# A four-layer transformer on one core: the second stack's first norm as a factor, other orders around the splits

## The chip, the cores and the metric

The kernel runs on one core of a Trainium2 chip. The metric is the device time of one execution in microseconds (us); lower is better. A second time that stands here is the span of one profiled execution, from the first to the last instruction on the core.

Five engines work side by side, each in its own order: TensorE (PE; its weight loads are PEld), VectorE (DVE), ScalarE (ACT), GpSimd (POOL) and the queue that starts most transfers, SyncE (SP).

## The reference, cut to what matters

256 tokens of width 1024 go through two stacks of two layers each. All weights are float32.

```
for i in (0, 1):                       # first stack, DEPTH = 2
    mix = token_mixers(x, w_in[i], ...)          # two attentions, gates ga, gb, then w_out
    x = layer_norm(ALPHA * x + mix, ln1)
    ffn = hierarchical_moe(x, ...)               # 32 experts, 2 of them for each token
    ple = sigmoid(x @ w_ple_gate[i]) * (p[i] @ w_ple[i])
    x = layer_norm(ALPHA * x + ffn + ple, ln2)
for l in (0, 1):                       # second stack
    h = rms_norm(x, attn_norm[l])
    x = x + hybrid_mixer(h, w_in_2[l], ...)      # cq, mq, mk, mv, rq, rk, rv; gates g0, g1, g2, rg
    h = rms_norm(x, mlp_norm[l])
    x = x + squared_relu_mlp(h, w_mlp_up[l], w_mlp_down[l])
return rms_norm(x, final_norm)
```

`rms_norm(x, g)` is x times a factor of the token, rsqrt(mean(x*x) + eps), times g of the column. A product of it with a matrix is therefore the product of x*g with the matrix, times the factor of each token (row).

## The kernel before, in words

**Blocks and splits.** The weights come as blocks of at most 128x2048 numbers, 1 MB. SP starts each block's transfer (line 1045) into a free buffer: three rings, and at times parts of other tiles that are lent (H, V, PT, GT, and YA and YB, which are parts of A). SP works its list in order, so a transfer whose buffer is not free holds up all later ones. Each block but those of `w_exp_down` is then split into a high and a low half: ACT casts it to WSh (line 1971), DVE subtracts and writes WSl (line 1406), both in two pieces. PE multiplies high by high, high by low and low by high, three matmuls where one would do (`mm3`, line 1060 is the call of all of them). There are three pairs of WSh and WSl, so two blocks can be split ahead of the one that PE works on.

**The plan.** All engines walk the same list of steps, written by `Plan`; each picks its own part of each step. `take` puts the transfer and the split of a block and of up to two blocks that follow into the list (`limit` caps how many), then the step that uses it. Small DVE steps (`spare`: the top-k search of the index attention, the routing) are dealt out `pace` at a time behind each `take`, `lead` at a time ahead of it. `fill` puts deferred blocks (`todo`: mostly the gates) between parts of an attention, so that PE has matmuls while softmax runs.

**Activations** are kept transposed for PE: XTh and XTl, 8 chunks of 128 columns by 256 tokens. `turn_split` fills them: four groups of four PE transposes (line 1156), each of two chunks, go to a PSUM bank each; where the vector along the columns is only a scale (`SCALED`), ACT writes the high halves (line 2066) and DVE the low ones (line 1659); with scale and shift (`SHIFTED`: ln1, ln2, o2) the two engines share the scaled copies first, then split them. There are four banks in turn, and a bank is free when the step that reads it has been done by its owner.

**The end of the first stack** (layer 1): `scatter` adds the experts' output to X on DVE, with the statistics (lines 1387, 1389); `normed` of ln2 writes H; `overflow` is a branch (line 936) that is only entered when an expert has over 64 tokens: PE waits for the last addition, then compares; `spread` has PE broadcast gain and shift of ln2; `affine` (lines 1729, 1732) makes X from H on DVE; `load_c2` fetches rope tables. `normed` of attn takes statistics of X and writes H again (lines 1364 to 1379, POOL's power at 2208, then 1720 and ACT's 2097), `turn_split` of attn transposes that, and `wide` of cq (416 columns) begins the second stack. In its layer 1 the same `normed` and `turn_split` stand behind the last `mlp_down` block, whose four PSUM quarters are done by token half, then by column half.

**The second stack's projections** follow in the order cq, mq, ct's transposes, mk, q_up, kv_up, mv, QT's transposes, rv, KT's transposes (line 1139), rope of mq, rq, rope of rq, then the attentions mla, moba and ret with the gates between. The staged copies of the wide products are ACT's (line 1993).

**Attention of the first stack** (`attend`, diff): scores of token half 0, softmax (exponentials: ACT, line 2020), a `fill` of a gate block, then `mix` on DVE (lines 1561 to 1570), scores of half 1, transposes of half 0's probabilities (line 1183), softmax of half 1, and so on.

**Ahead of the experts**: `ln1` is normed right behind w_out, three `ple` products stand between it and its transposes; then six blocks of gate and router (`parts`) with the routing dealt out, `ranks` (PE counts, DVE lines 1808 to 1818), `slots` (DVE lines 1824 to 1836, the gather matrix G), `spread` and `affine` of ln1 for both token halves, eight `gather` products whose banks ACT empties (line 2115), and `tokens_of` for expert 0 (ACT 2122, DVE 1856). H, which `affine` reads, is then lent as the first buffer for the experts' weights: SP waits at that transfer for the `affine` of half 1. The late steps of the routing and `kept` (DVE lines 1769 to 1852) stand behind the last gather. Each expert is two split blocks, one `down` block that is not split (32 matmuls with 64 columns), and `turn_h` (transposes at line 1279, DVE 1869 to 1873, ACT 2136).

## Time and profile before

| | us |
|---|---|
| median of 3 runs | 2013.76 |
| lowest and highest | 2011.25, 2013.92 |
| the profiled execution's own time | 2016.33 |
| its span | 2014.2 |
| its mean granted TensorE clock | 0.975 of full |

A profile has a busy time for each engine, a chain of waits that ended last, and groups of instructions by line; the trace behind it has every instruction with its start, its length and, in brackets, how long its engine had been idle before it and who released it. Line numbers are those of the kernel before. Where PE has a gap, the row that ends it says whom it waited for; "issue" means that nothing in the profile held it.

### The profile page before, as it was taken

How to read it: one execution, taken by the hardware profiler on the slowest of the kernel's cores; microseconds unless marked ns; L12 is line 12 of the kernel's file. 1: busy time of each engine (PE TensorE's matmuls, PEld its weight loads, DVE VectorE, ACT ScalarE, POOL GpSimd, SP SyncE). 2: the span in 40 equal slices, each digit the busy share in tenths (PEclk: the TensorE clock that was granted, in tenths of full speed). 3: DMA queues.
4: the chain of work that ended last, by engine and by line, in shares of the span. 5: the costliest groups of instructions: out<-in, count | busy, mean ns of one | idle time of the engine just before them, and what ended most of it. 6: DMA issues, size and time to landing. Idle time of an engine off the chain costs nothing.

```text
span 2014.2 us, 31129 instructions
## 1 busy us (share of the span) xinstructions
PE 1908.9 (95%) x12576; PEld 1746.1 (87%) x12576; DVE 1406.5 (70%) x2285; ACT 1073.4 (53%) x1680; POOL 65.7 (3%) x78
## 2 busy tenths in 40 slices
PE   7899989999989999899998799999999999999998
PEld 6789879989878898799897689998998889998997
DVE  5876779888669767788886666676445666676444
ACT  5454557777544545677774445445444544444442
POOL 1000000000000000000000000000000000000001
PEclk9999989999899999899998899999999999999999
DMA  7426169999544252799993343445555343345552
GB/s 290 138 84 232 58 244 404 384 407 421 214 167 148 105 218 72 305 404 373 421 421 149 115 167 115 152 153 174 199 189 184 131 157 137 126 176 180 188 189 84
DMA packets 61049, 426.76 MB, mean 212 GB/s; under 512 B 6960, under 2 KB 7088, under 8 KB 11872
## 3 DMA queue, kind: packets, MB, share of 16 engines
q1 hardware_dynamic: 59760, 421.65, 55.5%
q8 instruction: 104, 1.70, 0.3%
q0 software_dynamic: 416, 1.81, 0.3%
q10 hardware_dynamic: 720, 1.19, 0.2%
q14 instruction: 49, 0.40, 0.1%
HBM read 423.58 MB, written 1.05 MB: 211 GB/s over the span
## 4 chain that ended last, share of the span: by engine, by line
PE 78%; DVE 13%; ACT 4%; DMA 3%; issue 1%; POOL 1%; DVEq 0%; ACTq 0%; SPq 0%; POOLq 0%
PE bank L1060 63%; PE scp L1060 10%; DVE WSl L1406 4%; ACT WSh L1971 1%; PE bank L1279 1%; PE bank L1156 1%; ACT SC L2020 1%; DMA PT<-wts 1%; DMA H<-wts 1%; PE bank L1139 1%; DVE sm L1554 1%; POOL sm L2208 1%; PE bank L1183 1%; PE bank L1299 1%; DMA A<-wts 1%
## 5 line engine op out<-in xcount | busy, mean ns | idle before, releaser
L1406 DVE TENSOR_TENSOR WSl<-ring,WSh 128x1024 fp32r<-128x1024 f32 (+3 forms) x512 | 590.3, 1197 | 203.4 <-ACT WSh L1971 202.1
L1971 ACT CAST WSh<-ring 128x1024 fp32r<-128x1024 f32 (+3 forms) x512 | 499.2, 1029 | 191.0 <-PE bank L1060 98.2
L1060 PE MATMUL bank<-XTh,WSh 128*128 128x256 f32 x1216 | 349.6, 288 | 7.2 <-DVE A L1589 4.4
L1060 PE MATMUL bank<-XTl,WSh 128*128 128x256 f32 x1216 | 345.9, 284 | 0.0
L1060 PE MATMUL bank<-XTh,WSl 128*128 128x256 f32 x1216 | 345.8, 284 | 0.0
L1060 PE MATMUL bank<-WSh,FA 128*128 128x512 f32 (+1 forms) x848 | 303.5, 391 | 6.2 <-DVE FA L1863 6.1
L1060 PE MATMUL bank<-WSl,FA 128*128 128x512 f32 (+1 forms) x680 | 263.2, 387 | 0.0
L1060 PEld LDWEIGHTS bank<-XTh,WSh 128*128 128x128 f32 x1216 | 234.9, 193 | 9.6 <-issue 5.4
L1060 PEld LDWEIGHTS bank<-XTl,WSh 128*128 128x128 f32 x1216 | 235.2, 193 | 0.2
L1060 PEld LDWEIGHTS bank<-XTh,WSl 128*128 128x128 f32 x1216 | 234.9, 193 | 0.0
L1060 PE MATMUL bank<-WSh,XTh 128*128 128x512 f32 (+4 forms) x544 | 204.2, 375 | 14.3 <-DVE WSl L1406 11.1
L1060 PE MATMUL bank<-WSh,XTl 128*128 128x512 f32 (+4 forms) x544 | 201.4, 370 | 0.0
L1060 PE MATMUL bank<-WSl,XTh 128*128 128x512 f32 (+4 forms) x544 | 201.4, 370 | 0.0
L1060 PEld LDWEIGHTS bank<-WSh,FA 128*128 128x128 f32 x848 | 158.0, 190 | 39.4 <-DVE FA L1863 7.7
L1060 PE MATMUL scp<-WSh,FA 128*128 128x512 f32 x512 | 159.3, 389 | 0.0
L1060 PEld LDWEIGHTS bank<-WSl,FA 128*128 128x128 f32 x680 | 129.1, 190 | 24.2
L1060 PEld LDWEIGHTS bank<-WSh,XTh 128*128 128x128 f32 x544 | 105.1, 193 | 30.1 <-DVE WSl L1406 11.3
L1060 PE MATMUL bank<-FA,WSh 128*128 128x256 f32 x640 | 118.2, 287 | 0.0
L1060 PEld LDWEIGHTS bank<-WSh,XTl 128*128 128x128 f32 x544 | 104.8, 193 | 14.1
L1060 PEld LDWEIGHTS bank<-WSl,XTh 128*128 128x128 f32 x544 | 105.1, 193 | 13.4
L1060 PEld LDWEIGHTS scp<-WSh,FA 128*128 128x128 f32 x512 | 96.1, 188 | 19.9
L1060 PEld LDWEIGHTS bank<-TMP,ring 128*128 128x128 f32 x896 | 104.3, 192 | 2.2
(285 smaller groups left out, 2906.8 us busy)
## 6 DMA issues: line engine op xcount, KB each, us to landing
ring<-wts SPq DMA_DIRECT2D x264, 1024.0 KB, 4.9
V<-wts SPq DMA_DIRECT2D x40, 1024.0 KB, 12.4
PT<-wts SPq DMA_DIRECT2D x30, 1024.0 KB, 9.1
H<-wts SPq DMA_DIRECT2D x28, 1024.0 KB, 9.5
GT<-wts SPq DMA_DIRECT2D x12, 1024.0 KB, 13.2
A<-wts SPq DMA_DIRECT2D x8, 1024.0 KB, 7.5
ring<-wts SPq DMA_DIRECT2D x8, 584.0 KB, 7.1
ring<-wts SPq DMA_DIRECT2D x4, 832.0 KB, 7.7
```

The lines of the kernel that those rows point to most:

```text
L1060: return nc.tensor.matmul(dst, lhsT, rhs, start=start, stop=stop)
L1139: last = nc.tensor.transpose(bank[u % 4][0:s.w, j * P:(j + 1) * P], src, ident)
L1156: last = nc.tensor.transpose(bank[u % 4][:, j * P:(j + 1) * P], src(t, c), ident)
L1183: last = nc.tensor.transpose(bank[u % 4][:, (j - s.first) * P:(j - s.first + 1) * P], p_at(j // nk)[:, j % nk * P:(j % nk + 1) * P], ident)
L1279: last = nc.tensor.transpose(bank[u % 4][:, f * P:(f + 1) * P], SE[s.e % 2][:, f * P:(f + 1) * P], ident)
L1299: last = nc.tensor.transpose(bank[u % 4][:, j * P:(j + 1) * P], YC[:, 4 * s.n + j, s.j * P:(s.j + 1) * P], ident)
L1406: nc.vector.tensor_tensor(lo[:, c], buf[:, c], hi[:, c].bitcast(F32), ALU.subtract).then_inc(*lo_done.inc(("block", i)))
L1554: nc.vector.tensor_reduce(mx[:, h], scp[:, h, 0:kl], AX.X, ALU.max).then_inc(*dve_done.inc())
L1971: nc.scalar.copy(hi[:, c], buffers[s.buffer][:, c]).then_inc(*hi_done.inc(("half", i, k)))
L2020: ins = nc.scalar.activation(SC[:, h, 0:kl], scp[:, h, 0:kl], ACT.Exp, bias=nb[t][:, h:h + 1], scale=SCALE[s.name], accum_out=zs[t][:, h:h ...
L2208: nc.gpsimd.tensor_tensor(var, var, const("nhalf")[:, 0:groups], ALU.pow).then_inc(*pool_done.inc(("pow", *name)))
```

## The change

- **The factor.** For the second stack, `normed` and the scaled H are gone from the way into cq. In layer 0, `at0` transposes the H of ln2 and applies ln2's gain and shift times the attn gain (made by a step `columns`); in layer 1, `attn` transposes X itself. The factor of the tokens (`rms`) is computed beside the products and applied by ACT in its staged copies. `affine` of ln2 is put around the first cq block.
- **A second set of transposes.** The gates can't take a factor of the tokens, as they are made transposed; so a step `scaled` writes X times the factor to H (DVE half 0, ACT half 1), and after rq `at2` transposes H and refills XT for all that follows. KT's transposes move behind it, rope of mq ahead of rq.
- **mlp_down** of second-stack layer 0 ends by column half, then token half; the statistics of its additions move into `rms`.
- **overflow**: PE's and ACT's waits move inside the branch. `load_c2` no longer waits for `affine`.
- **keep_on**: four 256-column matmuls whose result is not used, ahead of the last `down` of each expert stage.
- **Slots and mixing**: `mix` of half 0 goes ahead of the fill; the splits of expert 0's blocks go behind `slots`; `affine` of ln1 is parted, half 1 behind the fourth gather and expert 0's first `tokens_of`; the late routing and `kept` go behind `turn_h` of expert 0; two `ple` products and their copies go ahead of ln1's `normed`, one stays behind it; `pace` is 3, not 8, during dv.

```diff
@@ Plan @@
+        self.ahead(i, spec)                # in take(); the body of ahead() is take()'s own loop, unchanged
...
+    def keep_on(self, n):
+        self.add("keep_on", n=n, u=self.bank("pe"))
...
         if att == "diff":
-            self.fill(fills[0])
             self.add("mix", name=att, l=l, t=0)
-        else:
-            self.fill(fills[0])
+        self.fill(fills[0])
...
         self.columns("w_in", "dk", l, W1["dk"], 512, src)
         self.add("rope", name="dq", l=l)
+        self.pace = 3
         self.columns("w_in", "dv", l, W1["dv"], 512, src)
...
-        self.add("normed", name="ln1", l=l, n=D)
+        self.limit = 0
         i = self.take(("w_ple", (l,), 0, 2, 0, D))
+        self.limit = 3
...
-        for c in range(3):
+        for c in range(2):
             ple(c)
+            ple_out(c)
+        self.add("normed", name="ln1", l=l, n=D)
+        self.ahead(i, self.specs[i])
+        ple(2)
         xt = self.use("XT", "pe")
-        ple_out(0)
-        ple_out(1)
...
+            self.limit = 0 if c >= 4 else 3
             blocks[c]()
...
         self.add("slots", l=l, i=i, p=self.use("P", "pe"))
+        self.limit = 2
+        self.ahead(len(self.specs) - 1, self.specs[-1])
+        self.limit = 3
         self.add("spread", name="ln1", l=l, scp=self.use("scp", "dve"))
-        self.affine("ln1", l)
+        self.affine("ln1", l, (0,))
...
-            if k == KD - 1:
-                for n in ROUTE_LATE:
...
-                self.add("kept", l=l)
+            if k == 3:
+                self.affine("ln1", l, (1,))
...
             self.add("turn_h", l=l, e=e, u=self.bank("dve"))
+            if e == 0:
+                for n in ROUTE_LATE:
...
+                self.add("kept", l=l)
             self.spread_out(1)
         self.pace = 1
+        self.keep_on(4)
         self.down(l, NE - 1)
@@ second_layer @@
-        self.add("normed", name="attn", l=l, n=D)
-        self.turn_split("attn", l, KD, xt=self.use("XT", "pe"))
-        for f in self.wide(w, "cq", l, 0, W2["cq"], W2["mq"] - W2["cq"], src):
-            f()
+        xt = self.use("XT", "pe")
+        self.turn_split("attn" if l else "at0", l, KD, xt=xt)
+        blocks = self.wide(w, "cq", l, 0, W2["cq"], W2["mq"] - W2["cq"], src)
+        if l == 0:
+            self.add("spread", name="ln2", l=DEPTH - 1, scp=self.use("scp", "dve"))
+            self.affine("ln2", DEPTH - 1, (0,))
+            blocks[0]()
+            self.affine("ln2", DEPTH - 1, (1,))
+            self.add("rms", l=l)
+        else:
+            self.add("rms", l=l)
+            blocks[0]()
+        blocks[1]()
...
         self.columns(w, "rv", l, W2["rv"], 512, src)
+        self.add("rope", name="mq", l=l)
+        self.add("scaled", l=l)
+        blocks = self.wide(w, "rq", l, 0, W2["rq"], 512, src, xt=xt)
+        blocks[0]()
+        blocks[1]()
+        self.turn_split("at2", l, KD, xt=self.use("XT", "pe"))
+        src = ("at2", l)
         self.turn("KT", l, 16, 96)
-        self.add("rope", name="mq", l=l)
-        self.columns(w, "rq", l, W2["rq"], 512, src)
@@ PE @@
+                elif s.kind == "keep_on":
+                    bank_free(u)
+                    for _ in range(s.n):
+                        last = mm(bank[u % 4][:, 0:256], ident, CST[:, 0:256], True, True)
...
                 elif s.kind == "overflow":
-                    for v in range(u - 4, u):
-                        pe.wait_ge(emptied(v), "bank", v)
-                    pe.wait_ge(dve_done, "added", "moe", l, 1, 1)
-                    overflow_tensor(e, l, yes)
+                    overflow_tensor(e, l, yes, u)
@@ DVE @@
+                elif s.kind == "rms":
+                    if l:
...
+                    for t in range(T):
+                        if l == 0:
+                            dve.wait_ge(dve_done, "affine", "ln2", DEPTH - 1, t)
+                        norm_stats(X[:, t:t + 1, :], 1, D, 160 + 2 * t, NORM_EPS, True, ...)
+                elif s.kind == "scaled":
+                    dve.wait_ge(pool_done, "pow", "attn", l, 0)
+                    nc.vector.tensor_scalar(H[:, 0, :], X[:, 0, :], RMS[:, 0, 1:2], None, ALU.mult)...
@@ ACT, staged copies of the wide products @@
-                        nc.scalar.copy(STAGED[s.name][:, t, ...], bank[u[t] % 4][:, 0:s.n])...
+                        dst, scale = STAGED[s.name][:, t, ...], 1.0
+                        if s.src[0] == "attn":
+                            act.wait_ge(pool_done, "pow", "attn", l, t)
+                            scale = RMS[:, t, 1:2]
+                        nc.scalar.activation(dst, bank[u[t] % 4][:, 0:s.n], ACT.Copy, scale=scale)...
```

## Rows read from the trace of the kernel before

**Rows 1.** The chain of waits that ended last: its share by engine (page)
```profile
PE 78%; DVE 13%; ACT 4%; DMA 3%; issue 1%; POOL 1%; DVEq 0%; ACTq 0%; SPq 0%; POOLq 0%
```

**Rows 2.** PE's waits over the span: engine, line, waited for: us in total, times, longest
```profile
PE bank L1183 <- DVE SC L1570: 5.3, 2, 2.6
PE bank L1060 <- DVE A L1589: 4.4, 1, 4.4
PE bank L1156 <- ACT GT L2104: 3.7, 2, 1.8
```

**Rows 3.** Stretches at the lower clock: length, busy time of each engine, granted clock, DMA
```profile
286.30:293.10 6.80, 4.34 (x12) 3.29 (x13) 6.07 (x9) 2.72 (x4) 0.00 (x0) 0.50 1.01 425
535.50:545.70 10.20, 9.43 (x46) 9.24 (x45) 2.25 (x3) 3.33 (x5) 0.00 (x0) 0.50 0.17 65
1078.20:1091.80 13.60, 12.57 (x58) 12.41 (x59) 3.34 (x6) 4.12 (x7) 0.00 (x0) 0.50 0.33 138
1102.10:1122.50 20.40, 7.56 (x30) 7.22 (x31) 14.01 (x31) 6.22 (x12) 2.86 (x5) 0.50 0.06 15
1562.90:1569.70 6.80, 4.16 (x19) 4.16 (x20) 3.73 (x13) 4.33 (x10) 1.30 (x2) 0.50 0.00 0
```

**Rows 4.** PE into the second stack's layers: start, length, operation, idle before
```profile
1104.96 2.07 PE L1060 MATMUL scp<-PR,PICK 128*128 128x256 f32 x8 [4.97 <-DVE H L1722]
...
1117.01 3.65 PE L1156 MATMUL bank<-CST,H 128*128 128x128 f32 x16 [9.98 <-ACT H L2097]
...
1565.54 3.65 PE L1156 MATMUL bank<-CST,H 128*128 128x128 f32 x16 [6.44 <-ACT H L2097]
```

**Rows 5.** PE's branch, and PE behind it at first-stack layer 0's end
```profile
L936 PEldq COMPARE_BRANCH  x2: 3421/3454/3486, 556.0 to 1101.5; - x2
...
559.68 1.09 PE L1156 MATMUL bank<-CST,H 128*128 128x128 f32 x4 [5.15 <-ACT H L2100]
562.62 2.82 PE L1156 MATMUL bank<-CST,H 128*128 128x128 f32 x12 [1.86 <-issue]
...
566.61 0.29 PE L1060 MATMUL bank<-WSh,XTh 128*128 128x292 f32 x1
```

**Rows 6.** ACT and DVE filling XT, affine, the copies ahead of mk
```profile
1118.13 3.40 ACT L2066 ACTIVATE XTh<-bank,PC 128x256 fp32r<-128x256 f32 x8 [0.66 <-PE bank L1156]
...
1119.01 3.43 DVE L1659 SCALAR_TENSOR_TENSOR XTl<-bank,PC,XTh 128x256 fp32r<-128x256 f32 x8 [2.94 <-ACT XTh L2066]
...
1106.32 1.22 DVE L1729 SCALAR_TENSOR_TENSOR X<-H,scp 128x1024 f32<-128x1024 f32 x1 [2.21 <-PE scp L1060]
...
1111.17 1.27 DVE L1364 BATCH_NORM_STATS2 sm<-X 128x6 f32<-128x512 f32 x2
...
1144.24 0.47 PE L1060 MATMUL bank<-WSh,XTh 128*128 128x512 f32 x1 [2.01 <-ACT A L1993]
```

**Rows 7.** SP ahead of the experts: its wait, the first transfer behind it, both layers
```profile
SPq L1045 <- DVE X L1732: 33.3, 2, 17.1
...
276.57 0.33 SPq L1045 DMA_DIRECT2D H<-wts  x1
...
819.64 0.33 SPq L1045 DMA_DIRECT2D H<-wts  x1
```

**Rows 8.** The same stretch on DVE, ACT and PE
```profile
809.05 2.36 DVE L1406 TENSOR_TENSOR WSl<-A,WSh 128x1024 fp32r<-128x1024 f32 x2 [0.53 <-ACT WSh L1971]
...
816.06 3.53 ACT L2115 ACTIVATE A<-bank,PC 128x512 f32<-128x512 f32 x4 [1.91 <-PE bank L1060]
...
824.38 2.01 ACT L1971 CAST WSh<-H 128x1024 fp32r<-128x1024 f32 x2 [0.65 <-DMA H<-wts]
...
832.68 0.79 PE L1060 MATMUL bank<-WSh,FA 128*128 128x512 f32 x1 [2.11 <-DVE FA L1863]
```

**Rows 9.** A down block at the lower clock (the last) and at full clock
```profile
1078.47 7.06 PE L1060 MATMUL bank<-TMP,PT 128*128 128x64 f32 x32 [1.87 <-DVE TMP L1873]
...
295.16 3.68 PE L1060 MATMUL bank<-TMP,ring 128*128 128x64 f32 x32
```

**Rows 10.** KT's or QT's transposes: an ACT copy of one group
```profile
1174.70 0.58 ACT L2030 COPY A<-bank 96x512 f32<-96x512 f32 x1
```

**Rows 11.** One step of the top-k search on DVE; PE's first product behind it
```profile
85.60 0.42 DVE L1537 MAX8 sm<-TMP 128x8 f32<-128x256 f32 x1
...
95.01 0.43 PE L1060 MATMUL bank<-XTh,WSh 128*128 128x256 f32 x1 [4.43 <-DVE A L1589]
```

**Rows 12.** Layer 0's diff attention: last exponential, the split that follows, softmax of half 1
```profile
110.27 0.21 ACT L2020 ACTIVATION_READ_ACCUMULATOR SC<-scp,sm 128x1 f32 x1
...
111.45 2.36 DVE L1406 TENSOR_TENSOR WSl<-ring,WSh 128x1024 fp32r<-128x1024 f32 x2 [2.51 <-ACT WSh L1971]
...
116.57 0.69 DVE L1552 TENSOR_TENSOR scp<-scp,CST 128x512 f32<-128x512 f32 x1
```

More of the change, by code:

```diff
@@ L181, in take, with ahead @@
         self.specs.append(spec)
+        self.ahead(i, spec)
+        self.spread_out(self.pace)
+        return i
+    def ahead(self, i, spec):
         order = self.order
@@ L196, in take @@
                 self.give_back(j)
-        self.spread_out(self.pace)
-        return i
     def release(self, i):
@@ L247, in turn_split @@
         pairs = range(2 * at, 2 * at + n, 2)
-        if name not in ("ln1", "ln2", "o2"):
+        if name not in ("ln1", "ln2", "at0", "o2"):
             for j in pairs:
@@ L473, in first_layer @@
                 self.down(l, e - 1)
+            if e == NE - 1 and l == DEPTH - 1:
+                self.add("columns")
             if e == NE - 1:
@@ L498, in first_layer @@
             self.turn_split("ln2", l, KD, xt=self.use("XT", "pe"))
-        self.add("spread", name="ln2", l=l, scp=self.use("scp", "dve"))
-        if l == DEPTH - 1:
-            self.affine("ln2", l)
+        if l < DEPTH - 1:
+            self.add("spread", name="ln2", l=l, scp=self.use("scp", "dve"))
     def down(self, l, e):
@@ L868, in build @@
                  "ct": (CTS, lambda t, c: CS[:, t, c * P:(c + 1) * P]),
[L869 to L871 removed]
+                 **{n: (XT, lambda t, c: H[:, t, c * P:(c + 1) * P]) for n in ("ln1", "ln2", "at0", "at2")},
+                 **{n: (XT, lambda t, c: X[:, t, c * P:(c + 1) * P]) for n in ("attn", "mlp")}}
+        SCALED = {"oa": lambda l, c: col("diff_subln_g", l, 0), "attn": lambda l, c: col("attn_norm_2", l, c), "at2": lambda l, c: col("attn_norm_2", l, c),
                   "mlp": lambda l, c: col("mlp_norm_2", l, c),
@@ L933, in overflow_pool, with overflow_tensor @@
                 pool.wait_ge(over[l]["dve"], "end", l)
-        def overflow_tensor(e, l, yes):
+        def overflow_tensor(e, l, yes, u):
             with e.If(yes > 0):
                 pe, o_pe = Waiter(e), over[l]["pe"]
+                for v in range(u - 4, u):
+                    pe.wait_ge(emptied(v), "bank", v)
+                pe.wait_ge(dve_done, "added", "moe", l, 1, 1)
                 def free(n):
@@ L1101, in tensor_program @@
                         if t == T - 1:
-                            names += [("read", i)] + ([("FA", s.fa)] if s.name == "w_out" and s.h else [])
+                            names += [("read", i)] + ([("FA", s.fa)] if s.name == "w_out" and s.h else [("XT", s.xt)] if s.name == "rq" and s.h else [])
                         if names:
@@ L1144, in tensor_program @@
                         pe.wait_ge(dve_done, "x_out", DEPTH + l, s.j // 2)
-                    elif s.name in ("ln1", "ln2", "attn"):
+                    elif s.name == "attn":
+                        for t in range(T):
+                            pe.wait_ge(dve_done, "y", "mlp", l - 1, s.j // 2, t)
+                    elif s.name == "at2":
+                        pe.wait_ge(dve_done, "scaled", l)
+                        pe.wait_ge(act_done, "scaled", l)
+                    elif s.name == "at0":
+                        pe.wait_ge(dve_done, "normed", "ln2", DEPTH - 1, s.j // 2)
+                        pe.wait_ge(act_done, "normed", "ln2", DEPTH - 1, s.j // 2)
+                    elif s.name in ("ln1", "ln2"):
                         pe.wait_ge(dve_done, "normed", s.name, l, s.j // 2)
@@ L1329, in tensor_program @@
                     ends = s.q == 3 and s.c == 3
-                    for n, t in [(n, t) for t in range(T) for n in range(2)] if ends else [(n, t) for n in range(2) for t in range(T)]:
+                    for n, t in [(n, t) for t in range(T) for n in range(2)] if ends and l == DEPTH - 1 else [(n, t) for n in range(2) for t in range(T)]:
                         for k in range(2):
@@ L2225, in gpsimd_program @@
                     power(4, 64, ("weighted", s.name, l, t))
+                elif s.kind == "rms":
+                    for t in range(T):
+                        power(1, 160 + 2 * t, ("attn", l, t))
                 elif s.kind == "normed":
@@ L2242, in gpsimd_program @@
                 elif s.kind == "load_c2":
-                    pool.wait_ge(dve_done, "affine", "ln2", DEPTH - 1, 1)
+                    pool.wait_ge(pe_done, "scatter", DEPTH - 1, 1, 1)
                     e.dma_start(CST[:, C_N:C_N + C2_N], consts[P * (C_N + C1_N):P * (C_N + C1_N + C2_N)].rearrange("(p n) -> p n", p=P)).then_inc(
```

62 lines of the change are left out of this document (45 added, 17 removed).

## The prediction

> **What bounds the kernel now.** I read the chain of waits first: PE has 78% of it, DVE 13%, ACT 4% [rows 1]. The end is set by PE's stream of products and by the places where DVE or ACT hold it. So I went through PE's gaps with their releasers [rows 2, 4, 5], then the stretches at half clock [rows 3] and at what a product loses there. Last I read SP's wait ahead of the experts [rows 7], because the change moves a step that this wait hangs on. About 0.2% (4.0 us) is what a measurement of this kernel can tell from no change.
>
> The sum is made on the profiled execution, 2016.33 us, which lies 2.57 above the median; it is taken off at the end.
>
> **1. dv's pace.** In layer 0 DVE works through top-k steps (0.46 each with the replace, [rows 11]) while PE waits 4.4 for its copies [rows 2]. Some 11 fewer stand ahead of them: the copies come right behind the split, 2.4 earlier, and the block behind the gap no longer starts at half clock (0.43 for a product that later takes 0.28, [rows 11]): 1.5. In layer 1 eight left-over steps fall ahead of other copies: +0.8. Together -3.1; ends: both gaps closed, -5.9, or the steps only moved, +1.
>
> **2. Mixing ahead of the fill.** PE's two 2.6 waits are for DVE's mixing of half 0 [rows 2]. The last exponential ends at 110.5, DVE is then idle until the split at 111.45 and starts softmax of half 1 at 116.57 [rows 12]. With mixing (some 2.9) first, split second, softmax comes at 115.8, 0.75 earlier, and then ACT's exponentials of half 1 are what is late next. So -0.75 in each layer, -1.5. Ends: both waits gone, -5.3; the split delays PE as much as it gains, +1.
>
> **3. ln1.** Two ple copies go ahead of the norm, so ACT's XT copies stand behind one, not three: the 1.8 waits for ACT [rows 2] shrink by 0.7 each, -1.4. Ends -3.6 and 0.
>
> **4. Slots, affine, routing.** `slots` no longer waits behind a split (2.36, [rows 8]), but two casts of 2.0 on ACT and two splits of 2.36 now stand ahead of ACT's gather copies and of `affine`. The first four gather copies, which end at 819.6 [rows 8], end near 822.0; tokens_of takes 0.5, `affine` of half 1 2.4 [rows 6]. SP issues the H transfer straight behind that `affine` (819.64, [rows 7]), so now at 825.0, 5.4 later; everything queued behind it on SP waits as long. Expert 1 starts 13.0 behind that issue (832.68, [rows 8]): transfer, cast at 824.38 [rows 8], splits; 1.6 of it was late routing ahead of the splits, which leaves: +3.7. The late routing (2.8) now stands behind `turn_h` of expert 0, where the next splits wait for it: +0.7. Layer 1: +4.5. In layer 0 the issue goes from 276.57 [rows 7] to 281, the routing gives back 1.9: +3.2, of which a shorter wait at `ranks` is part. Together +7.5. Ends: DVE's and SP's slack absorb it, 0; nothing absorbs it and the clock falls besides, +16. I take the middle because expert 1 already starts on a DVE wait [rows 8]: there is no slack at its own place, but 30 experts follow in which SP can only win time back where it waits for buffers.
>
> **5. keep_on.** Ahead of the last `down` PE idles 1.87 and then runs it at 0.50: 7.06 against 3.68 [rows 9]; the stretches are 10.2 and 13.6 long [rows 3]. Eight passes of some 0.21 (half of a 0.43 for the same width at half clock, [rows 11]) fit into that idle time, so they cost nothing; were the gap shorter, they would cost 1.7. If the clock holds, -3.4 in layer 1 and, by the same rows, -2.4 in layer 0: -5.8. Ends: -5.8 and 0. Both falls begin at that gap, so I take the full effect, and give the other its own case.
>
> The Trainium skill, "TensorE: Matmul & The Clock Gate", section "Why this matters for your kernels", has the clock fall only behind waits a good deal longer than this one. The trace shows falls that begin at 1.9 of idle, so it does not agree; by the rule those eight passes change nothing, and this term is 0. That is rival (b).
>
> **6. The branch.** PE's compare takes 3.42 to 3.49 [rows 5], behind DVE's last addition. It now starts when the scatter's products end, 1.5 earlier (554.5, not 556.0); the 5.15 idle in layer 0 [rows 5] shrinks, -1.3 (the 1.86 of "issue" behind it, code arriving, stays). Ends -1.5, 0. In layer 1 it lies inside term 7.
>
> The Trainium skill, "Advanced Engine Details and Errata", section "Control Flow Timing", gives a compare-and-branch about 108 ns. The trace has 30 times that. By the page this term would be 0.
>
> **7. Into the second stack, layer 0.** Now 4.97 idle, 2.07 of spread, 9.98 idle, then the transposes, 3.65, at half clock [rows 3, 4]: PE waits for spread, four `affine` parts of 1.2 (1106.32, [rows 6]), statistics (1.27 from 1111.17, [rows 6]) and scaling. After: the transposes follow on ln2's H itself, near 1105, and are written in the form with a shift, which in layer 0 took 559.68 to 566.61 with a hole of 1.9 [rows 5]: 5.1 to 5.6, so the first product comes at some 1110.6, not 1120.3 (3.3 behind the transposes' start at 1117.01). From there to mk, now at 1144.24 behind a wait for ACT's copy [rows 6], are 23.9. That stretch grows: DVE's `affine` halves (4.9 by [rows 6]) and the statistics now lie in it among the splits, and ACT's copies of cq wait for the factor; I put 3.3 of it on PE, two thirds of the `affine`. mk starts near 1137.8: -6.4. Ends: all 9.7 and the 2.0 wait in part, -10.8; -5.
>
> **8. Layer 1.** Statistics, power and scaling cost 6.44 idle [rows 4], at half clock [rows 3]. The transposes of X need none: they start at 1559.1. The stretch of 6.8 at half clock ends earlier, but the factor must be there for ACT's first copy, some 6 later, which it is. -7.1. Ends: 6.44 plus 1.7 of clock, -8.1; -5.5.
>
> **9. at2.** 16 more transposes are 1.83 at full clock (half of 3.65, [rows 4]). They cost more than that: ACT's eight copies take 3.40, DVE's eight 3.43 [rows 6], and the last low half ended 5.4 behind the first transpose, 4.9 at full clock. KT's groups, which used to lie between rv and rq with work beside them, now wait for those banks; their last copy (0.58, [rows 10]) ends some 5.9 behind the start of at2, and the scores wait for it. KT's own 1.9 is gone from its old place: +4.0 in each layer, +8.0. Ends: PE time alone, +1.9 each; 5.5 each and 1.7 of clock, +14.4.
>
> **10. Small.** Scaled ACT copies where exposed: +0.3. `scaled` (DVE 1.0, ACT 1.3 by its width, the affine row's 1.22), `columns`, `load_c2`: beside rv's and rq's products; without that cover some 1.3 per layer.
>
> **Sum**: -3.1 -1.5 -1.4 +7.5 -5.8 -1.3 -6.4 -7.1 +8.0 +0.3 = -10.8; 2005.5 on the profiled time, **2003.0** against the median.
>
> **Rivals.** (a) *Larger gain.* at2 costs its PE time only (4.2 less) and both mixing waits close (3.8 less): 18.8 off, 1995.0. For it: DVE is off PE's chain through most of rq. Against: the bank order ahead of the scores.
> (b) *keep_on buys nothing*, as the clock falls for a reason that lies ahead of the gap (the 10.2 and 13.6 stretches include `down`'s small products, [rows 3], where PE is busy 92%): the sum is -5.0, 2008.8. For it: idle of 1.9 occurs in many places with no fall. Against: both falls start at that very gap.
> (c) *Slower.* The experts pay in full: H's issue 5.4 late, routing 2.8 and a longer stretch at half clock as in 286.3 to 293.1 [rows 3], 1.7 to 3.4: 9.9 to 11.6 in each layer, 19.8 to 23.2 in place of 7.5: 2015.3 to 2018.7. It decides from 18.3 in both. For it: SP's list is in order, and it already waits 17.1 and 16.2 there [rows 7]. Against: in layer 0 `ranks` gives 1.5 back, and the routing had stood in expert 0's way before.
>
> **Chances**: forecast 0.48, (a) 0.20, (b) 0.22, (c) 0.06, the rest 0.04 spread about. Faster than 2009.7: all of the first two and over half of (b), 0.81; slower than 2017.8 only in (c) and odd mishaps, 0.06; else 0.13. The bounds that stand widest are terms 4 (8.5), 9 (6.4) and 5 (5.8) upward, 4 (7.5), 7 and 9 (4.3 each) downward; in few cases all go together: 1993.5 to 2011.5, which leaves out most of (c).
>
> **What the changed kernel's profile would show.** Term 5: `down` of expert 31 at 3.7 and no stretch at 0.50 there. Term 9: PE waits for ACT or DVE at KT's transposes and at the first scores, some 4 in all. Term 4: H's transfer some 5 behind the old place, and expert 1 late by 3 to 4. Terms 7 and 8: no wait on H; a wait for ACT's staged copies ahead of mk. Term 1: 2.0 left of the 4.4. Wrong would be: experts delayed by over 9 per layer, at2's block over 6, or a new wait of PE for the factor in cq's banks.

## The result, and the profile after

The changed kernel takes 1992.29 us (median; 1990.44 to 1994.07 in four runs), the kernel before beside it 2013.84. The ratio is 0.9889, with a 95% interval of 0.9865 to 0.9912: faster by 1.1%, about 21.5 us. The forecast was 10.8 off and 2003.0; the time lies 1.2 below its range. Measured again in five runs it was 1993.13, ratio 0.9896 (0.9876 to 0.9916). The profiled execution of after takes 1992.25, its span is 1990.4, 23.8 less than before's.

The page of after, the chain of waits by engine, answers to [rows 1]: PE has three points more.

```profile
PE 81%; DVE 13%; ACT 3%; DMA 1%; issue 1%; POOL 0%; DVEq 0%; ACTq 0%; SPq 0%
```

The waits of PE in the trace of after (engine, line, waited for: us in total, times, longest) answer to [rows 2]:

```profile
PE bank L1097 <- DVE WSl L1459: 17.0, 4, 10.7
PE bank L1330 <- ACT SC L2227: 15.0, 2, 7.5
PE bank L1207 <- DVE H L1793: 9.2, 4, 4.2
PE bank L1234 <- DVE SC L1623: 5.5, 4, 1.8
PE bank L1097 <- DVE A L1642: 0.8, 1, 0.8
```

The waits of 10.0 and 6.4 for the scaled H are gone. DVE's copies during dv hold PE's products once, for 0.8, where the wait was 4.4. The mixing of layer 0's and 1's attention (line 1623) still costs 5.5 in all: it was 5.3. The first row was 11.1 in two waits before; two of 3.5 and 2.3 on the way into the second stack, for DVE's splits, are new in it. The second row, 7.5 in each layer ahead of `turn_h` of expert 0, was this before:

```profile
PE bank L1279 <- ACT SC L2140: 6.1, 2, 3.1
```

Five of the nine stretches at the lower clock after the change, columns as in [rows 3]:

```profile
277.10:287.30 10.20, 4.61 (x12) 3.52 (x13) 8.33 (x25) 7.28 (x9) 0.00 (x0) 0.50 1.02 430
550.20:553.60 3.40, 3.40 (x18) 3.40 (x17) 2.63 (x5) 2.83 (x7) 0.00 (x0) 0.50 0.01 2
816.40:823.20 6.80, 3.92 (x11) 2.97 (x12) 6.21 (x21) 5.13 (x7) 0.00 (x0) 0.50 1.01 428
1086.00:1089.50 3.50, 3.50 (x19) 3.50 (x18) 2.29 (x4) 3.10 (x7) 0.00 (x0) 0.51 0.22 68
1116.80:1120.20 3.40, 3.16 (x8) 2.52 (x9) 3.30 (x6) 3.22 (x7) 0.00 (x0) 0.50 0.75 214
```

The two of 10.2 and 13.6 around the last `down` do not occur; the 20.4 on the way into the second stack has become 3.5 and 3.4, and the 6.8 ahead of its layer 1 is gone. The mean granted clock is 0.989 instead of 0.975: by span times (1 - clock) times two, an estimate, 44 us at half clock instead of 101. This is more than the terms of the prediction had counted.

To see where the 23.8 came from I set the starts of the same PE groups of both traces side by side (after minus before, and the change of that from stage to stage):

| stage (start of its last group, before) | shift | change | forecast |
|---|---|---|---|
| first matmuls to the index scores (64.8) | +0.57 | +0.6 | |
| top-k, dv, transposes, layer 0 (102.4) | -4.56 | -5.1 | -3.9 |
| diff attention, layer 0 (170.8) | -6.06 | -1.5 | -0.75 |
| ln1 to the first product of `ranks` (261.6) | -6.96 | -0.9 | -0.7 |
| `ranks` to expert 2's first product (299.0) | -5.81 | +1.2 | +3.2 |
| experts, layer 0 (532) | -6.30 | -0.5 | 0 |
| last `down`, transposes, scatter (547.0) | -9.72 | -3.4 | -2.4 |
| branch, XT (566.6) | -13.55 | -3.8 | -1.3 |
| layer 1 to the end of diff attention (697) | -13.42 | +0.1 | 0 |
| ln1 to `ranks` (805.7) | -14.49 | -1.1 | -0.7 |
| `ranks` to expert 2 (841.8) | -12.0 | +2.5 | +4.5 |
| experts, layer 1 (1076) | -13.73 | -1.7 | 0 |
| `down` to scatter (1092.5) | -18.59 | -4.9 | -3.4 |
| into the second stack, mk's products (1155.2) | -25.71 | -7.1 | -6.4 |
| at2, layer 0 (1199.4) | -21.07 | +4.6 | +4.2 |
| MLP into layer 1 (1589.3) | -28.75 | -7.7 | -7.1 |
| at2, layer 1 (1645.1) | -23.92 | +4.8 | +4.2 |

Terms 3, 7, 8 and 9 came as forecast to within 0.7 in each row. Four did not: 4, 5, 6 and 1, all in the same direction.

How far one profile can be trusted is seen from the second profile of the changed kernel, set against the kernel before in the same way. Its stages agree with these to 0.2, but for four: the start is 1.5 earlier, layer 0's diff attention gains 0.8 more, the last `down` to the scatter of layer 0 gains 1.0 less, and layer 1 to the end of its diff attention gives back 1.6, not 0.1. In the last two a stretch of 3.5 at half clock (from 529.9 and from 591.3) stands in one profile and not in the other. The three rows of at2 and of the MLP into layer 1 are the steadiest: in the nine other profiles with the same steps there they come again to within 0.06.

### The profile page after: what moved, and what is told of

Its sections match the earlier page's. It is cut to its first block, busy times and chain, and to the rows that moved or that the text cites. A ratio compares the mean times of both kernels' runs of the same rounds, so it can differ in the third digit from the quotient of the medians.

```text
span 1990.4 us, 31257 instructions
## 1 busy us (share of the span) xinstructions
PE 1901.8 (96%) x12624; PEld 1731.5 (87%) x12624; DVE 1410.8 (71%) x2301; ACT 1078.4 (54%) x1694; POOL 67.1 (3%) x78
## 4 chain that ended last, share of the span: by engine, by line
PE 81%; DVE 13%; ACT 3%; DMA 1%; issue 1%; POOL 0%; DVEq 0%; ACTq 0%; SPq 0%
PE bank L1097 67%; PE scp L1097 11%; DVE WSl L1459 4%; PE bank L1330 1%; ACT SC L2102 1%; ACT WSh L2049 1%; PE bank L1207 1%; DVE sm L1607 1%; DMA ring<-wts 1%; PE bank L1234 1%; PE bank L1176 1%; DVE scp L1605 1%; POOL sm L2294 0%; DVE XTl L1712 0%; DVE sm L1412 0%
```

## The experiments

All runs are set against the kernel before on the same chip, whose median was 2012.06, 2012.52, 2012.39 and 2013.61 in the four groups of runs. The intervals of the ratios reach 3 to 5 us to either side, so a difference of 2 or 3 us between two runs is not settled by their times; there the traces have to say where it lies.

**keep_on taken out of the changed kernel.**

```diff
-        self.keep_on(4)
         self.down(l, NE - 1)
```

> The changed kernel without keep_on. Theory 'the clock is held': the four unused matmuls keep the granted clock at full through the last down, the transposes and the scatter, so without them both stretches at 0.50 return (10 to 14 us long) and the end of each first-stack layer is later by 3.4 and 4.9 us, +8.3 in all: about 2000.6 against 1992.3. Theory 'they only fill a gap' (the clock falls or holds for other reasons): no change, 1992.3 within 1 us. Forecast's own size of the term: +5.8, 1998.1.

2000.39 (1999.29 to 2000.83), ratio 0.9934 (0.9918 to 0.9951): 8.1 slower, as the first theory has it. Its stretches around the last `down` (windows: length, busy time by engine, clock) and layer 1's `down` in PE's timeline:

```profile
527.80:534.60 6.80, 6.03 (x29) 5.84 (x29) 1.23 (x2) 2.32 (x4) 0.00 (x0) 0.50 0.06 24
1067.10:1080.80 13.70, 12.94 (x61) 12.75 (x62) 3.77 (x6) 4.71 (x7) 0.00 (x0) 0.50 0.30 124
```

```profile
1066.95 6.92 PE L1096 MATMUL bank<-TMP,PT 128*128 128x64 f32 x32 [1.87 <-DVE TMP L1943]
```

The `down` takes 6.92 again, behind the same idle 1.87. In the changed kernel it is this:

```profile
1062.70 1.89 PE L1097 MATMUL bank<-CST 128*128 128x256 f32 x8
1064.73 3.76 PE L1097 MATMUL bank<-TMP,PT 128*128 128x64 f32 x32
```

Each of the four matmuls shows as two passes. The eight passes take the place of the wait, and `down` takes 3.76. The stretch at half clock held the transposes behind `down` too, and they give the 2.5 that the forecast left out.

The step does not hold the clock every time. Of the fourteen profiles of kernels with it, none has a stretch at half clock from layer 1's last `down` to the end of the scatter; in layer 0 three have one of 3.4 in the transposes behind `down`, the second profile of the changed kernel among them. This is its window:

```profile
529.90:533.30 3.40, 3.33 (x16) 3.33 (x17) 1.36 (x2) 1.86 (x4) 0.00 (x0) 0.50 0.00 0
```

Its stage gains 2.45 on the kernel before, not 3.41.

**keep_on alone, in the kernel before** (the same step, ahead of its last `down`).

> The kernel before with keep_on alone. Theory 'the step works by itself': 8 us off, as its removal from the changed kernel gave, 2004.3. Theory 'it needs the rest of the change' (a neighbouring wait lets the clock fall all the same): less than 4 us off, over 2008.

2007.26, ratio 0.9969 (0.9957 to 0.9981): 6.3 less than the 2013.61 beside it, by the medians. The stage from `down` to scatter came 3.40 and 4.85 earlier than in the kernel before, the same as the 3.42 and 4.86 of the whole change. It works by itself. That the medians give 2 less than 8.3 is within their spread (2005.58 to 2013.30 here, 2010.38 to 2020.12 for the kernel before).

**The third part undone**: splits of expert 0 ahead of `slots`, `affine` whole, late routing behind the last gather.

```diff
-            self.limit = 0 if c >= 4 else 3
...
-        self.limit = 2
-        self.ahead(len(self.specs) - 1, self.specs[-1])
-        self.limit = 3
...
-        self.affine("ln1", l, (0,))
+        self.affine("ln1", l)
...
-            if k == 3:
-                self.affine("ln1", l, (1,))
+            if k == KD - 1:
+                for n in ROUTE_LATE:
...
+                self.add("kept", l=l)
...
-            if e == 0:
-                for n in ROUTE_LATE:
...
-                self.add("kept", l=l)
```

> The changed kernel with the third part undone: splits of expert 0's blocks ahead of slots again, affine of ln1 whole ahead of the gathers, late routing and kept behind the last gather. As the forecast had it (this part costs 7.5 us): about 1984.8. Theory read from the changed trace (H's transfer 2.7 to 3.7 later than before, seen from ranks, 1.5 to 1.8 given back by the routing, and the product block ahead of gather at full clock, 4.1 in place of 5.7): it costs 3.7, so 1988.6. Theory 'it pays': over 1992.3.

1990.01, ratio 0.9886 (0.9870 to 0.9903): 2.3 less than 1992.29. By the ratios it is 0.6 to 2.0 less, as one takes 0.9889 or 0.9896 for the changed kernel. So the part costs some 1 to 2 us, not 7.5; that it costs anything is not clear of the noise by the times.

**Halves of it.** Only the splits back ahead of `slots`:

> The changed kernel with only the splits of expert 0's blocks back ahead of slots (affine stays parted, late routing stays late). Theory 'ACT's two casts ahead of its gather copies are what delays H': H's transfer 2.7 (layer 0) and 3.7 (layer 1) earlier, against which the wait at ranks (1.4, layer 0) and the product block ahead of gather at half clock (1.6 in each) may come back: 1990 to 1991, the 2.3 of the run with all of it undone or a little less. Theory 'the parted affine and the late routing cost it': 1992.3.

1994.98, ratio 0.9906 (0.9891 to 0.9921): 2.7 slower than 1992.29 and 1.8 slower than 1993.13, which neither theory had. In its trace expert 2 starts when it did, to 0.3; the profiled time is lost elsewhere, 1.4 of it in a stretch at half clock from 594.0, which five of the other profiles have too.

Only `affine` and the routing back:

> The changed kernel with only affine of ln1 whole and the late routing behind the last gather again (splits stay behind slots). Theory 'the routing ahead of the splits costs, the affine's place does not': H's transfer 0.4 earlier, expert 1 1.6 later behind it, so 1.2 slower in each layer, 1994.7. Theory 'the parted affine delays H': faster than 1991.

1992.27, ratio 0.9896 (0.9881 to 0.9911): no change. The first theory's 2.4 did not come.

What the two halves do is seen from when H's transfer is issued, when expert 1 and when expert 2 start, each counted from the first product of `ranks` (layer 0 / layer 1, worked out from the starts in the traces):

| | H issued | expert 1 | expert 2 | product block ahead of gather |
|---|---|---|---|---|
| before | 14.93 / 13.91 | 28.24 / 26.95 | 37.40 / 36.08 | 5.66 / 5.65 |
| after | 17.62 / 17.62 | 29.12 / 29.15 | 38.55 / 38.58 | 4.08 / 4.09 |
| all undone | 14.57 / 13.91 | 27.85 / 26.90 | 37.33 / 36.73 | 5.67 / 4.09 |
| splits undone | 17.77 / 17.80 | 29.06 / 29.43 | 38.48 / 38.85 | 4.09 / 4.09 |
| affine and routing undone | 17.28 / 17.28 | 28.61 / 28.80 | 37.69 / 38.73 | 4.09 / 4.09 |

Either half alone holds H back by 2.7 to 3.9: with `affine` parted, its second half waits for ACT's copies of the first four gathers whatever the splits do; with the splits in front of it, it stands behind their 4.6 on DVE. Undoing one therefore wins next to nothing; undoing both wins 3.0 and 3.7 at H's issue, of which 1.2 and 1.9 are left at expert 2.

The row "before" is one execution, and for layer 1 an early one. The kernels with keep_on alone and with the branch alone have the order of before here, and their expert 2 starts at 36.96 / 38.91 and 38.75 / 36.22. The mean of the three is 37.7 and 37.1. The nine profiles with the order of after have 38.4 to 39.0 and 38.5 to 39.2, but for layer 0 of the next run (41.9). So the 3.7 that the two profiles give for this part is some 2.5 when all are taken together, which fits the 1 to 2 of the runs. What lies between H's issue (2.7 to 3.0 and 3.5 to 3.7 later against each of the three) and expert 2 differs by up to 2.8 between executions of one order.

**The clock held ahead of expert 0's `turn_h`.**

```diff
+            if e == 0:
+                self.keep_on(14)
             self.add("turn_h", l=l, e=e, u=self.bank("dve"))
```

> The changed kernel with fourteen more unused matmuls in PE's wait of 7.5 us ahead of turn_h of expert 0 (both layers). Theory 'the clock is what is left there': the stretches at 0.50 of 10.2 and 6.8 us go, and turn_h and the products of expert 1 (5.6 and 5.3 us) take 4.2: about 2.3 off in each layer, 1987.8. Theory 'the splits set the pace there': expert 1 waits for DVE instead, 1992.3 within 1 us. Theory 'in the way': the matmuls end behind the H block's split and delay turn_h: slower than 1992.3.

1997.11, ratio 0.9918 (0.9902 to 0.9935): 4.8 slower. PE in layer 1 of this kernel, then two of its windows:

```profile
812.91 6.21 PE L1099 MATMUL bank<-CST 128*128 128x256 f32 x28
820.55 0.66 PE L1332 MATMUL bank<-CST,SC 128*128 128x128 f32 x4 [1.43 <-ACT SC L2229]
822.11 0.50 PE L1099 MATMUL bank<-WSh,FA 128*128 128x512 f32 x1 [0.91 <-DVE FA L1936]
...
825.91 3.68 PE L1099 MATMUL bank<-TMP,ring 128*128 128x64 f32 x32
...
831.54 0.69 PE L1099 MATMUL bank<-WSh,FA 128*128 128x512 f32 x1 [1.50 <-DVE FA L1936]
```

```profile
813.00:820.00 7.00, 6.11 (x29) 5.04 (x27) 3.27 (x3) 3.98 (x5) 0.00 (x0) 1.00 1.00 421
824.00:831.50 7.50, 6.04 (x46) 5.43 (x44) 7.26 (x22) 4.57 (x7) 0.00 (x0) 1.00 1.02 426
```

The clock held: expert 1's products take 4.0, not 5.3. But expert 2 starts 38.55 behind `ranks` (after: 38.58): what expert 1 wins, expert 2 waits. It waits for DVE, which is busy for 7.26 of the 7.50 us of the second window. The late routing, which the change put behind `turn_h` of expert 0, is done first there (from 823.57 to 826.26), then two splits and the tokens of expert 2:

```profile
826.26 2.35 DVE L1461 TENSOR_TENSOR WSl<-ring,WSh 128x1024 fp32r<-128x1024 f32 x2
828.53 2.35 DVE L1461 TENSOR_TENSOR WSl<-PT,WSh 128x1024 fp32r<-128x1024 f32 x2
830.80 0.69 DVE L1936 TENSOR_TENSOR FA<-A,FA 128x512 fp32r<-128x512 f32 x1
```

The start of expert 1 does hang on the transfers, which are busy all the time, at 421 to 426 GB/s: ACT's copy that `turn_h` needs stands behind the casts of H and of the block after it, and both wait for their data. This is ACT in layer 0 of this kernel:

```profile
276.06 1.99 ACT L2051 CAST WSh<-H 128x1024 fp32r<-128x1024 f32 x2 [5.48 <-DMA H<-wts]
279.83 1.99 ACT L2051 CAST WSh<-ring 128x1024 fp32r<-128x1024 f32 x2 [1.78 <-DMA ring<-wts]
281.73 0.58 ACT L2229 COPY SC<-bank 128x512 f32<-128x512 f32 x1
```

In layer 0 the filled 6.2 us were followed by a wait of 2.6 and the clock was at half all the same. Of the 4.8, 3.3 is lost up to expert 2 in layer 0 (41.89 behind `ranks`, not 38.55): 1.6 is the product block ahead of gather at half clock (5.7 in place of 4.1), and ACT's wait for the block after H is 1.3 longer (1.78, not 0.47). Another 1.6 is a stretch at half clock from 831.7 in layer 1. So the first theory falls: the transfers set when expert 1 starts, DVE when expert 2 does. The clock held with the late routing back in its old place was not run; it would show whether DVE is what takes the gain away.

**The branch.** PE's waits ahead of it again:

```diff
-                for v in range(u - 4, u):
-                    pe.wait_ge(emptied(v), "bank", v)
-                pe.wait_ge(dve_done, "added", "moe", l, 1, 1)
...
                 elif s.kind == "overflow":
+                    for v in range(u - 4, u):
+                        pe.wait_ge(emptied(v), "bank", v)
+                    pe.wait_ge(dve_done, "added", "moe", l, 1, 1)
                     overflow_tensor(e, l, yes, u)
```

> The changed kernel with PE's waits ahead of the branch again. Theory 'only the start moves': each layer's end later by the 1.5 us between the last scatter product and the last addition, +3.0 in all, 1995.3. Theory 'code arrives in the idle time too': in layer 0 also the hole of 1.9 marked issue comes back and with it a stretch at half clock, +3.8 in layer 0 and 1 to 1.5 in layer 1, +5, about 1997.4.

1995.71 (1994.20 to 1998.65), ratio 0.9917 (0.9899 to 0.9934): 3.4 slower, between the two. Its runs overlap with the changed kernel's nine (1990.44 to 1995.76), so the size is loose; the trace shows the mechanism. Where the branch stands, first here, then PE around it in layer 0 (timeline), then both for the changed kernel:

```profile
L969 PEldq COMPARE_BRANCH  x2: 3751/3788/3826, 544.2 to 1082.1; - x2
```

```profile
548.11 3.65 PE L1204 MATMUL bank<-CST,H 128*128 128x128 f32 x16 [5.42 <-ACT H L2187]
```

```profile
L969 PEldq COMPARE_BRANCH  x2: 3382/3604/3826, 540.6 to 1077.2; - x2
```

```profile
541.01 3.79 PE L1097 MATMUL scp<-FA,OHT 128*128 128x512 f32 x16
549.00 1.17 PE L1207 MATMUL bank<-CST,H 128*128 128x128 f32 x9 [4.20 <-DVE H L1793]
```

In the changed kernel the branch begins at 540.6, while PE's products go on until 544.8: it is done before they are, and its 3.4 cost nothing. With the waits in front it begins at 544.2, takes 3.8 and ends when the transposes start; the idle time is 5.42. The 1.9 of "issue" is seen in neither, so the second theory's hole did not come back, and why it stood in the kernel before stays open.

**The branch alone, in the kernel before.**

> The kernel before with PE's waits inside the branch alone. Theory 'PE's sequencer runs ahead and fetches the code beside the scatter's products': in layer 0 the idle times of 5.2 and 1.9 us become one of about 4.2 and the stretch at half clock shrinks, 3.8 off; in layer 1 PE's next work waits 5.0 for H and then for affine, so 0 to 1.5 off there; 2008 in all. Forecast's theory 'the branch only starts when the last product ends': 1.3 off, 2011.

2009.05, ratio 0.9971 (0.9959 to 0.9983): 4.6 less than 2013.61 and 1 more than forecast by the first theory. Layer 0's idle time is 4.20, and the stage is 3.0 shorter:

```profile
551.25 3.79 PE L1063 MATMUL scp<-FA,OHT 128*128 128x512 f32 x16
559.24 1.09 PE L1159 MATMUL bank<-CST,H 128*128 128x128 f32 x4 [4.20 <-DVE H L1722]
```

In layer 1 `spread` comes 4.2 earlier behind the scatter and the transposes only 1.5, as the wait for the normed H is longer (13.47 instead of 9.98).

**The mixing of half 0 behind the fill again.**

```diff
-        if att == "diff":
-            self.add("mix", name=att, l=l, t=0)
-        self.fill(fills[0])
+        self.fill(fills[0])
+        if att == "diff":
+            self.add("mix", name=att, l=l, t=0)
```

> The changed kernel with mix of half 0 behind the fill again. Forecast's size of the term: 1.5 gained by the change, so 1993.8. Theory 'the wait only moved' (the trace after has two waits of 1.8 and 0.9 ahead of the transposes of half 0 where before had one of 2.6): 1992.3 within 1 us. Theory 'both waits closed': 1997.6.

1992.71, ratio 0.9895 (0.9879 to 0.9912): the same. In the changed kernel half 0's transposes start without a wait, and half 1's (not half 0's, as I had written) have two:

```profile
109.43 0.66 PE L1234 MATMUL bank<-CST,SC 128*128 128x128 f32 x4
```

```profile
119.51 0.66 PE L1234 MATMUL bank<-CST,SC 128*128 128x128 f32 x4 [1.83 <-DVE SC L1623]
121.08 1.11 PE L1234 MATMUL bank<-CST,SC 128*128 128x128 f32 x4 [0.91 <-DVE SC L1623]
```

1.83 and 0.91 are the old 2.6: DVE mixes half 1 behind ACT's exponentials (it idles 2.00 for them, up to 117.29), and only which transposes wait has changed. In this run the two waits of 2.6 are back.

**pace 8 again during dv.**

```diff
-        self.pace = 3
         self.columns("w_in", "dv", l, W1["dv"], 512, src)
```

> The changed kernel with pace 8 during dv. Forecast's size of the term: 3.9 in layer 0 and nothing given back in layer 1 (3.1 in all), 1995.4. Theory read from the changed trace (layer 0 gained 5.1 between the top-k search and the transposes, layer 1 nothing): 1997.4.

1999.63, ratio 0.9929 (0.9913 to 0.9946): 7.3 slower. In its trace the stage in layer 0 is 4.9 later, as read, and layer 1's is not; some 1.5 more is one stretch at half clock among the experts (367.3 to 370.7), which this run does not tie to the pace. So 4.9 is the part that the trace shows.

**KT's transposes back between rv and rq.**

```diff
         self.columns(w, "rv", l, W2["rv"], 512, src)
+        self.turn("KT", l, 16, 96)
...
         src = ("at2", l)
-        self.turn("KT", l, 16, 96)
```

> The changed kernel with KT's transposes between rv and rq again, at2 left where it is. Theory 'the order of the banks': of the 4.6 us that at2 costs in each second-stack layer only its own sixteen transposes (1.9) stay, as KT's sit beside products again and the scores need no bank of at2: 2.7 off in each, 5.4 in all, 1986.9. Theory 'the fill of XT holds the scores whatever the order': 1992.3 within 1 us.

1989.82 (1986.37 to 1992.72), ratio 0.9884 (0.9868 to 0.9901). The median is 2.5 less, not 5.4, and its four runs spread over 6.4 with the clock (0.990 at 1986.37, 0.985 at 1992.72), so the size is not settled by the times. The trace has it: PE from at2 to the scores, in the changed kernel and then here.

```profile
1171.87 1.91 PE L1207 MATMUL bank<-CST,H 128*128 128x128 f32 x16
1174.46 2.99 PE L1176 MATMUL bank<-CST,A 128*96 128x128 f32 x16 [0.68 <-DVE XTl L1712]
1178.32 2.02 PE L1097 MATMUL scp<-A 96*128 96x128 f32 x16 [0.87 <-DVE A L1642]
```

```profile
1172.04 1.91 PE L1207 MATMUL bank<-CST,H 128*128 128x128 f32 x16
1173.79 1.95 PE L1097 MATMUL scp<-A 96*128 96x128 f32 x16
```

The scores start 4.7 earlier behind at2; 1.8 of it is KT's own time, now among the products ahead. That leaves 2.9 in layer 0 and 2.8 in layer 1, and 0.4 and 0.9 of these are lost again in longer waits of the attentions behind. So it is some 4.4 in all. The profiled span is 6.0 shorter (1984.4 against 1990.4), but 1.6 of this was won ahead of the second stack, where the two kernels are the same.

**The two improvements together, and a third.**

> KT's transposes early and the third part undone, together. Theory 'they lie in different stages and add': 5.4 by the first (if its own run gives that) and the 2.3 measured of the second, 1984.6. Theory 'the chip gives back': over 1987.

1989.50 (1987.02 to 1994.43), ratio 0.9878 (0.9855 to 0.9901): they did not add by the median. The profiled run has 13 stretches at half clock, where the changed kernel has nine. One of the new ones, 3.4 from 1198.0, lies behind the moved scores; the next two kernels have it as well (from 1194.3 and 1190.6), and the MLP into layer 1 gives them 5.7 where the others have 7.7. KT's place alone did not show it.

Then eight unused matmuls behind the branch:

```diff
         self.add("overflow", l=l, u=len(self.owner))
+        self.keep_on(8)
```

> The changed kernel with KT's transposes early and eight unused matmuls (3.5 us) behind the branch, in PE's wait of 4.2 us for ln2's H, in both layers. Theory 'filled idle time keeps the clock': the stretches of 3.4 at half clock behind the branch go, 1.0 to 1.6 off in each layer beside what KT's place gives (3 to 5): 1985.5. Theory 'it does not matter, as in the wait ahead of expert 0's turn_h': as kt_early, about 1988.5.

1986.95 (1985.72 to 1988.55), ratio 0.9870 (0.9854 to 0.9885). The stretches at 550 and 1086 are gone. Against KT's place alone (0.9884) the intervals overlap.

> As the run before, and the third part (splits behind slots, affine parted, late routing) undone as well. If all three add: 2.3 less than that run, 1983 to 1986. If the third part's undoing gives the clock back elsewhere: equal to it within 1 us.

1983.56 (1978.24 to 1983.88), ratio 0.9844 (0.9829 to 0.9859): the best here, 8.7 below the changed kernel by the medians, 28.8 below the kernel before beside it.

**The changed kernel once more, as the base.**

> The changed kernel itself, beside the others. If the chips differ by what the kernel before showed in the calls (2012.1 to 2012.5 against 2013.8), 1991; else 1992.3. It is the base for the differences of the other runs.

1993.13, ratio 0.9896: not the 1991 that a quicker chip would have given. A difference of 1 us between groups of runs means nothing here.

No run undoes terms 3, 7 and 8; what is said of them rests on the table of stages alone.

## Why the prediction was wrong

The direction and the mechanisms of most steps were right; the sum was half of what came, because four terms were mis-sized the same way. (Its own working gives +7.6 for term 4, 3.2 and 4.4, where it writes +4.5 and +7.5; this changes nothing.)

- **Term 4**, +7.5, is the step that was off most: 3.7 in the two traces, some 2.5 over all of them, 1 to 2 by undoing it. H's issue came 2.7 and 3.7 later, not 4.4 and 5.4. The difference is the same 1.7 in both layers, and it is the product block between `ranks` and `slots`, which ran at half clock before and for which the forecast had no entry. In the new order ACT's casts stand behind that block, so its time goes into H's issue: where it took 5.66 in the new order (layer 0 of the run with the clock held ahead of `turn_h`), H was issued at 19.19, not 17.62. In the old order it does not: with all undone, layer 1 had 4.09 and H at 13.91, as before with 5.65. One of its three forms (line, engine, operation, shapes, count | busy us, mean ns), before and after:

```profile
L1060 PE MATMUL bank<-WSh,XTh 128*128 128x352 f32 x8 | 3.4, 424 | 0.0
```

```profile
L1097 PE MATMUL bank<-WSh,XTh 128*128 128x352 f32 x8 | 2.7, 335 | 0.0
```

  24 products in all, 5.7 in place of 4.1. Whether the block's full clock belongs to the part is open: with all of it undone layer 0 has 5.67 and layer 1 4.09, with the splits alone undone both have 4.09. The late routing's +0.7 per layer is not seen: expert 2 starts 20.9 and 21.0 behind H's issue, where it was 22.5 and 22.2. It is on DVE's path to expert 2 all the same, as the run with the clock held shows.
- **Term 5**, -5.8: measured 8.3 in the trace, 8.1 by taking it out, 6.3 alone; more than its own bound of -5.8. The step priced the `down` alone, while [rows 3] gave the whole stretch as 10.2 and 13.6 with PE 92% busy. Half of that busy time, 11.0, would have been too much. `down` gave 2.4 and 3.3, as priced; the 32 transposes behind it gave 1.0 and 1.6. At full clock they take 4.85 in layer 1 (from 1069.25, waits among them included), not half of the 6.40 before, because ACT's eight copies of their banks then follow each other without a gap:

```profile
1069.94 2.42 ACT L2238 ACTIVATE WSh<-bank,rt 128x512 fp32r<-128x512 f32 x4 [0.75 <-PE bank L1350]
1072.24 2.59 ACT L2238 ACTIVATE FA<-bank,rt 128x512 fp32r<-128x512 f32 x4
```

  Rival (b) is out. The rule of the Trainium skill ("TensorE: Matmul & The Clock Gate", section "Why this matters for your kernels") would have kept the clock up over so short a wait; with the four matmuls taken out it fell behind 1.87 of idle, in both layers, so the measurement decides against it here.
- **Term 6**, -1.3: measured 3.8 in layer 0, 3.4 in both by undoing, 4.6 alone. The sentence "It now starts when the scatter's products end" was wrong: without a wait in front, PE's sequencer reaches the branch 4 us before the products end. So the branch is off the path, and in layer 0 the idle 5.15 and 1.86 become one wait of 4.20 for ln2's H. That is 2.8 of the 3.8; the rest is a shorter stretch at half clock (3.4, not 6.8). The 1.86 of "issue" that I had left standing went too, for a reason that stays open. The 108 ns that the Trainium skill ("Advanced Engine Details and Errata", section "Control Flow Timing") gives a compare-and-branch are not what the trace has, 3.42 to 3.49 before and 3.38 to 3.83 after; the 0 that would follow from it for this term is wrong as well.
- **Term 1**, -3.1: 5.1 in layer 0 and nothing given back in layer 1, where I had +0.8; 7.3 by undoing, of which the trace ties 4.9 to it. The wait is now this:

```profile
91.96 0.36 PE L1097 MATMUL bank<-XTh,WSh 128*128 128x256 f32 x1 [0.81 <-DVE A L1642]
```

  0.8 is left of 4.4, where I had left 2.0.
- **Term 2**, -1.5: the runs give 0.4, which is no difference. It was right that the wait does not close, and why (softmax of half 1 is late next); the 0.75 per layer was still too much. The 1.5 in layer 0 of the table is clock: a stretch of 6.9 at half clock there where before had 3.4 and 6.8.
- **Term 9** was near: 4.6 and 4.8 with the scaled copies, against 4.2. The mechanism, KT's groups waiting for banks, is shown by the run that moves them: 1.7 and 2.0 of the 4.6 and 4.8 are left. **Terms 3, 7, 8** hold to 0.7 in each row. In term 7 there is luck in it: PE's first product of cq came 11.8 earlier, not 9.7, and mk started 8.6 earlier, not 6.4; 1.5 of that was given back by mk's own products at half clock (1116.8 to 1120.2), which the forecast did not have. The wait for ACT's staged copies ahead of mk, named as a sign, did not come; PE waits for DVE's split there, and longer than it had for the copies (3.5, not 2.0):

```profile
1117.04 0.77 PE L1097 MATMUL bank<-WSh,XTh 128*128 128x512 f32 x1 [3.51 <-DVE WSl L1459]
```

- Among the experts the kernel before lost 0.5 (425.2) and 1.7 (968.5 and 999.8). The two kernels made from it, keep_on alone and branch alone, did not, so these 2.2 of the 23.8 belong to its profiled execution, which lies 2.57 above the median, and not to the change.

Rival (a) named the outcome nearest (1995.0), but that was luck: neither mixing nor at2 was cheaper, which were its two reasons.

## What to carry to other kernels

Where PE runs at half clock, price every group in the stretch of the window's row, not only the one that starts it, each by what would hold it at full clock (here ACT's copies held the second one), and look for other groups nearby whose mean time is above that of the same form elsewhere. Profile the unchanged kernel twice before a stage of one profile is taken for an effect: stages with the same order differed by up to 2.8 us here. A wait in front of a branch costs more than its own length, as it keeps the sequencer from reaching the branch beside queued work. When a step is moved ahead of another, work out anew what that other hangs on: the way to H's issue led through DVE's split before, and through the product block and ACT's casts after.

## What the runs showed of the hardware

- PE's sequencer began a compare-and-branch of 3.4 us at 540.6, 4.2 us before the last of the queued products ended (541.01 plus 3.79), when no wait stood between them; no idle time was left from it.
- Eight unused passes (1.89 us in all) in a wait of 1.87 kept the granted clock at 1.00 up to the end of the scatter in all fourteen profiles in layer 1 and in eleven of fourteen in layer 0; in the kernel before 10.2 and 13.6 us there were at 0.50. 28 passes (6.2 us in all) in a wait of 7.5, with 2.6 of idle left behind them, did not keep it (layer 0); with 1.4 left they did (layer 1). Each of the two was seen once.
- With the clock at full, expert 1's products took 4.0 us and not 5.3, but PE won nothing by it: DVE, on which the next expert waited, was busy 7.26 of 7.50 us (the run with the clock held, layer 1).
- One and the same order of steps between `ranks` and expert 2 took 36.1 to 38.9 us in six stretches of three profiles (before, keep_on alone, branch alone).
- Executions of one and the same kernel differed by 6 us with the mean granted clock: 1986.37 at 0.990, 1988.53 at 0.989, 1991.11 at 0.986, 1992.72 at 0.985.
